# Other read places and directions for the feed-forward parts of a two-block transformer kernel

## The reference, cut to what matters

```python
# first block: 4 layers; mixers: retention, convolution, dilated attention, retention
x = x + _rmsnorm(m, norm_w[i, 1])
f = _swiglu(_rmsnorm(x, norm_w[i, 2]), ffn_w_in[i], ffn_w_out[i])   # hidden 2816
x = x + _rmsnorm(f, norm_w[i, 3])

def _swiglu(h, w_in, w_out):
    a = h @ w_in
    return (jax.nn.silu(a[..., :FFN_HIDDEN]) * a[..., FFN_HIDDEN:]) @ w_out

# second block: 2 layers on 16 + 256 = 272 tokens; mixers: mLSTM with LRU ("ab"), differential attention ("c")
h = h + mixer(_rmsnorm_2(h, norm_mix[layer]))
h = h + _sq_relu_mlp(_rmsnorm_2(h, norm_mlp[layer]), mlp_w1[layer], mlp_w2[layer])   # hidden 4096
```

## Time and profile before

| what | us |
|---|---|
| median of two timed runs | 2424.04 |
| lowest, highest | 2419.61, 2428.47 |
| span of the profiled execution | 2427.9 |
| instructions in it | 55624 |

### The profile page before, as it was taken

How to read it: one execution, slowest core, us unless ns; L and a number is a source line. 1 busy time by engine, 2 the same in 40 slices (tenths; PEclk the granted TensorE clock), 3 DMA queues, 4 the chain that set the end, 5 groups by cost and what they waited for, 6 DMA issues and landing times.

```text
span 2427.9 us, 55624 instructions
## 1 busy us (share of the span) xinstructions
PE 2388.4 (98%) x20004; PEld 2293.9 (94%) x20004; DVE 1705.2 (70%) x3359; ACT 1360.3 (56%) x2806; POOL 3.4 (0%) x9
## 2 busy tenths in 40 slices
PE   8999999999999999999999999999999999999998
PEld 8899999889999999999998999999899999999998
DVE  7667667877658777776576667657566775677764
ACT  5556555375555545565555555557755444566443
POOL 0000000000000000000000000000000000000000
PEclk9999999999999999999999999999999999999999
DMA  7535564336654444456555456644444555434564
GB/s 238 178 123 166 182 199 157 106 105 182 197 172 133 138 130 138 140 165 194 195 157 174 128 165 187 203 161 155 139 123 143 168 174 175 129 111 140 175 179 130
DMA packets 103400, 385.75 MB, mean 159 GB/s; under 512 B 11344, under 2 KB 13520, under 8 KB 103024
## 3 DMA queue, kind: packets, MB, share of 16 engines
q1 hardware_dynamic: 102784, 381.78, 50.5%
q0 software_dynamic: 496, 2.38, 0.3%
HBM read 383.07 MB, written 1.05 MB: 158 GB/s over the span
## 4 chain that ended last, share of the span: by engine, by line
PE 90%; DVE 6%; ACT 2%; issue 1%; DMA 0%; DVEq 0%; ACTq 0%; SPq 0%
PE acc L526 26%; PE acc L527 25%; PE acc L528 25%; DVE weights_lo L2155 2%; PE acc L732 1%; PE acc L733 1%; PE acc L734 1%; PE acc L754 1%; ACT weights_hi L1313 1%; PE acc L821 1%; PE acc L844 1%; PE acc L866 1%; DVE y L2293 1%; DVE h L2304 1%; PE acc L667 1%
## 5 line engine op out<-in xcount | busy, mean ns | idle before, releaser
L2155 DVE TENSOR_TENSOR weights_lo<-weights,weights_hi 128x512 fp32r<-128x512 f32 (+1 forms) x1392 | 907.0, 682 | 413.1 <-ACT weights_hi L1313 408.8
L526 PE MATMUL acc<-xn_parts,weights_hi 128*128 128x256 f32 (+1 forms) x3456 | 988.8, 286 | 14.3 <-DVE xn_parts L2300 6.8
L527 PE MATMUL acc<-xn_parts,weights_hi 128*128 128x256 f32 (+1 forms) x3456 | 974.7, 282 | 0.0
L528 PE MATMUL acc<-xn_parts,weights_lo 128*128 128x256 f32 (+1 forms) x3456 | 974.4, 282 | 0.0
L1313 ACT ACTIVATE weights_hi<-weights 128x512 fp32r<-128x512 f32 (+1 forms) x1392 | 815.6, 620 | 260.7 <-PE acc L528 230.8
L526 PEld LDWEIGHTS acc<-xn_parts,weights_hi 128*128 128x128 f32 x3456 | 653.7, 189 | 30.7 <-issue 21.8
L528 PEld LDWEIGHTS acc<-xn_parts,weights_lo 128*128 128x128 f32 x3456 | 652.3, 189 | 0.0
L527 PEld LDWEIGHTS acc<-xn_parts,weights_hi 128*128 128x128 f32 x3456 | 650.9, 188 | 0.9
L526 PE MATMUL acc<-arena_r,weights_hi 128*128 128x256 f32 (+1 forms) x1792 | 510.0, 285 | 3.6 <-DVE arena_r L2796 1.2
L528 PE MATMUL acc<-arena_r,weights_lo 128*128 128x256 f32 (+1 forms) x1792 | 506.3, 283 | 0.0
L527 PE MATMUL acc<-arena_r,weights_hi 128*128 128x256 f32 (+1 forms) x1792 | 506.2, 282 | 0.0
(11 more groups left out here) (325 smaller groups left out, 2324.5 us busy)
## 6 DMA issues: line engine op xcount, KB each, us to landing
weights<-in_ffn_in SPq DMA_DIRECT2D x176, 512.0 KB, 3.8
weights<-in_ffn_out SPq DMA_DIRECT2D x64, 704.0 KB, 4.1
weights<-in_att_in SPq DMA_DIRECT2D x72, 512.0 KB, 3.5
weights<-in_mlp_in SPq DMA_DIRECT2D x64, 512.0 KB, 3.5
weights<-in_mlp_out SPq DMA_DIRECT2D x64, 512.0 KB, 3.5
weights<-in_ret_qk SPq DMA_DIRECT2D x32, 512.0 KB, 3.7
weights<-in_ret_v SPq DMA_DIRECT2D x32, 512.0 KB, 3.6
weights<-in_ret_g SPq DMA_DIRECT2D x32, 512.0 KB, 3.6
```

The lines of the kernel that those rows point to most:

```text
L526: nc.tensor.matmul(acc, hi, src_hi, start=first, stop=False)
L527: nc.tensor.matmul(acc, hi, src_lo, start=False, stop=False)
L528: return nc.tensor.matmul(acc, lo, src_hi, start=False, stop=last)
L2155: nc.vector.tensor_tensor(w_lo[sub % phase.subs][:, 0:n, :], raw[slot][:, j * SUB:j * SUB + n, :], w_hi[sub % phase.subs][:, 0:n, :].bitca ...
```

## The change

The inputs of the feed-forward parts get places of their own, one for each layer, and six parts read them backwards.

```diff
-S2_STRIDE, MLP_AT, ARENA_PLACE = 320, 16, 832
+S2_STRIDE, ARENA_PLACE = 320, 832
+TURNED_INPUTS = ("ffn_in0", "ffn_out0", "ffn_in1", "mlp_in1", "mlp_out0", "mlp_out1")
+XN_AT = ((64, 64), (80, 80), (48, 80), (48, 96))
+XN2_AT = 48
+HIDDEN_AT = ((48, 48), (48, 48), (0, 16), (0, 32))
+MLP_AT = (0, 48)
...
-        xn_hi = {S1: chunks(xn_parts, 48, DC, S1), S2: chunks(xn_parts, 0, DC, S2_STRIDE)[:, :, 0:S2]}
...
+        def xn_place(number, half):
+            return (XN_AT[number // 2] if number % 2 else (48, 48))[half] + half * DC * S1
+
+        def xn_hi(number):
+            if number < 2 * DEPTH:
+                return chunks(xn_parts, xn_place(number, 0), DC, S1)
+            return chunks(xn_parts, 0, DC, S2_STRIDE)[:, :, XN2_AT:XN2_AT + S2]
...
-        hid_hi, hid_lo = chunks(arena_r, 0, FFN, S1), chunks(arena_r, FFN * S1, FFN, S1)
-        mlp_hi, mlp_lo = (chunks(arena_r, MLP_AT + n * MLP * S2_STRIDE, MLP, S2_STRIDE)[:, :, 0:S2] for n in range(2))
+        hid_hi = [chunks(arena_r, at[0], FFN, S1) for at in HIDDEN_AT]
+        hid_lo = [chunks(arena_r, at[1] + FFN * S1, FFN, S1) for at in HIDDEN_AT]
+        mlp_hi = [chunks(arena_r, at, MLP, S2_STRIDE)[:, :, 0:S2] for at in MLP_AT]
+        mlp_lo = [chunks(arena_r, at + MLP * S2_STRIDE, MLP, S2_STRIDE)[:, :, 0:S2] for at in MLP_AT]
...
-            def product(acc, hi, lo, src, first, last):
+            def product(acc, hi, lo, src, first, last, name=""):
                 src_hi, src_lo = src
+                if name in TURNED_INPUTS:
+                    acc, src_hi, src_lo = acc[:, ::-1], src_hi[:, ::-1], src_lo[:, ::-1]
                 nc.tensor.matmul(acc, hi, src_hi, start=first, stop=False)
```

More of the change, by code:

```diff
@@ L248, in chunks, with xn_lo @@
             return buf[:, at:at + n * t].rearrange("p (c t) -> p c t", t=t)
-        xn_hi = {S1: chunks(xn_parts, 48, DC, S1), S2: chunks(xn_parts, 0, DC, S2_STRIDE)[:, :, 0:S2]}
-        xn_lo = {S1: chunks(xn_parts, 48 + DC * S1, DC, S1),
-                 S2: chunks(xn_parts, DC * S2_STRIDE, DC, S2_STRIDE)[:, :, 0:S2]}
+        def xn_place(number, half):
[4 more added lines that the diff above has]
+            return chunks(xn_parts, 0, DC, S2_STRIDE)[:, :, XN2_AT:XN2_AT + S2]
+        def xn_lo(number):
+            if number < 2 * DEPTH:
+                return chunks(xn_parts, xn_place(number, 1), DC, S1)
+            return chunks(xn_parts, DC * S2_STRIDE, DC, S2_STRIDE)[:, :, XN2_AT:XN2_AT + S2]
         proj1 = chunks(arena, 0, 48, S1)
@@ L540, in multiply @@
                     last = product(acc, w_hi[sub % phase.subs][:, k % SUB, :], w_lo[sub % phase.subs][:, k % SUB, :], src(kk),
-                                   kk == 0, kk == phase.upo * phase.tiles - 1)
+                                   kk == 0, kk == phase.upo * phase.tiles - 1, phase.name)
                     if k % SUB == SUB - 1 or k == phase.tiles - 1:
@@ L597, in first_units @@
                         last = product(acc(u), w_hi[c % phase.subs][:, u, :], w_lo[c % phase.subs][:, u, :], src(c),
-                                       c == 0, c == DC - 1)
+                                       c == 0, c == DC - 1, phase.name)
                     last.then_inc(sub_multiplied, 1)
@@ L1269, in _ @@
                 gated_pairs(ph[f"ffn_in{layer}"], layer, src, ready)
-                src, ready = hidden(hid_hi, hid_lo, f"ffn_in{layer}")
+                src, ready = hidden(hid_hi[layer], hid_lo[layer], f"ffn_in{layer}")
                 dense_outputs(ph[f"ffn_out{layer}"], src, S1, ready)
@@ L1522, in chunk @@
                         act.wait_ge(x_ready, first - DC + c + 1)
-                    hi, value = xn_hi[S1][:, c, :], x[:, c, :]
+                    hi, value = xn_hi((k + 1) // 2)[:, c, :], x[:, c, :]
                     if residues:
@@ L2296, in rest @@
                     dve.wait_ge(xh_ready, DC * number + c + 1)
-                    lo, value, hi = xn_lo[S1][:, c, :], x[:, c, :], xn_hi[S1][:, c, :].bitcast(F32)
+                    lo, value, hi = xn_lo(number)[:, c, :], x[:, c, :], xn_hi(number)[:, c, :].bitcast(F32)
                     if residues:
@@ L2531, in unit @@
                     m = i * phase.body + u
-                    split_hidden(mlp_hi[:, m, :], mlp_lo[:, m, :], part[:, u % 2, :], i * phase.body, u, first)
+                    split_hidden(mlp_hi[int(phase.name[-1])][:, m, :], mlp_lo[int(phase.name[-1])][:, m, :], part[:, u % 2, :], i * phase.body, u, first)
                 stream(phase, unit)
```

20 lines of the change are left out of this document (10 added, 10 removed).

## The result

The kernel after takes 2444.39 us (2443.51 to 2445.27, two runs), the kernel before 2424.04 us; the ratio is 1.0080 with an interval of 1.0054 to 1.0107. It is slower by 20 us, inside the forecast range (2402 to 2458) and 16 us above the forecast of 2428.

A forecast was written before the change was run, and what follows sets the result against it. The prediction took TensorE's distance between matmul starts (121 ns over 20004 matmuls) to bound the kernel. Its terms 0 + 4 + 0 = +4 us on the median 2424.0 gave 2428 us, range 2402 to 2458 us.

The forecast's parts named there:

- (b): New places of the 272-column parts, 4800 matmuls: +0.8 ns each, +4 us, with ends of -24 and +7 us.
- (a): New places of the 256-column feed-forward parts, 6336 matmuls: a fresh draw of two levels, 0, with 14.6 us either side.
- they meet more often: Rival: in turned parts, moving and weight reads collide once more per matmul, +32 us, 2460 us; chance 0.15.
- the signs that the prediction named for being wrong: Turned or unequal-halves parts at their own level (turned 256 columns: below 112, above 119 ns), or 272-column parts at 64 falling towards 120.
- (c): Six parts read backwards, output too: 0 us, bounds from -9.7 and -11.8 us to near +496 us.
- No effect: Rival: places and direction don't matter, timing draws the levels of the parts; 2424 us, chance 0.15.
- The turned parts run free: Rival: turned ffn_in parts fall to 113.1 ns, turned MLP parts to 120.2; -21.5 us, about 2404 us; chance 0.18.
- Half pace: Rival: backward reading or writing in turned parts runs at half pace, (c)'s worst end, 2920 us; chance 0.07.

The follow-up runs named there:

- the experiment on the first block: Kernel after with the second block as before the change (forwards at 128), first block's places and directions kept: 2448.99 us, ratio 1.0112 to the kernel before.
- places alone: Kernel after with its new places but every part read forwards (no turned inputs): 2441.13 us, ratio 1.0082 to the kernel before.
- direction alone: Kernel after with its six parts still read backwards but all places put back as before the change: 2427.64 us, ratio 1.0030 to the kernel before.
- the backward map: Kernel after with all twelve feed-forward parts read backwards, at places 0, 64, 128 and 192 modulo 256 bytes; levels read, no time given.
- the padding: 64 bytes ahead of the weight buffers, against a kernel reading all parts forwards at 64; weights and xn shift, arena stays: 2432.34 us beside 2431.28 for the kernel before.
- the experiment on the rhythm: One plain f32 matmul heading each later ffn_in turn, added to the kernel with everything forwards at 64: 2417.71 us, ratio 0.9989 to the kernel before.

## Why the prediction was right or wrong

*The number* lies in the range and its sign is right, but that is in good part luck. Of the three terms of the sum, (b) had the wrong sign (+4 forecast, -5.6 measured in the two profiles), and (a), put at 0 with 14.6 us at most on either side, came to +19.4, outside its own bounds; the two misses partly cancel. That 2444 us fell inside 2402 to 2458 is owed to the room left for "they meet more often", whose mechanism did not occur. By the signs that the prediction named for being wrong, it was wrong: turned parts above 119 ns (120.0 in ffn_out0 and ffn_in1), a level of its own for halves at different places (118.7 in ffn_in3), and 272-column parts forwards at 64 down to 123.5 ns, part of the way towards 120.

*TensorE's distance between starts bounds the kernel, and nothing else moves*: right. Busy times, waits and clock of the other engines stayed, and every microsecond found is in that distance.

*Step (a), new places are a fresh draw with as many high as low, 0 us*: this step failed. I had seen that equal places show both levels and concluded that places don't matter. The runs show that both 113.3 and 117.8 ns were open at a distance of -64 bytes from the weights, and that the changed places held 117.8 to 120.0 ns in every long part. What it cost is all of the low parts and more: four parts from 113.3 to between 117.8 and 120.0 ns (+3.3 in ffn_out0, +2.6 in ffn_out1, +4.3 in ffn_in2, +5.2 us in ffn_in3, over their longest unbroken stretches), 0.6 and 2.1 us in ffn_in0 and ffn_in1, 19.4 us for the block in the two profiled executions. It is even more against the timed ones (27 to 29 us in the experiment on the first block). That fits a kernel before that is low in more parts in most of its runs than in the execution that I read: its medians of 2419 to 2420 us in the later measurements are close to the 2419.38 us of the execution with seven low parts. The levels of the timed runs themselves were not seen. That the profiled execution stood at the upper end of the timed pair was in the prediction; I did not ask what it was high by.

*Step (b), 272 columns +4 us*: wrong in sign. The price was taken from ab_out, whose chunks visit all four places (126.1 ns). That is within 0.6 ns of the mean of the four places (64 at 123.3, 128 at 125.3 or 126.7, 0 and 192 at 126.7); I used it for 64 alone. Measured: -5.6 us for the block, made of -1.8 ns a matmul in the parts that read forwards at 64, -0.3 to -0.4 ns in the two turned ones at 64, and 0 in mlp_out1.

*Step (c), direction 0 with bounds of -21.5 and +496 us*: right as a sum at the new places (places alone 1.0082, full change 1.0080), not as a rule. At the old places direction alone costs 1.0030, and seven out of seven long backward parts at 64 (three in that kernel, four in the backward map) stand on the high level.

*The rivals.* "No effect" fell: the padding moved levels as predicted by distance. "The turned parts run free" fell: none came below 117.8 ns. "They meet more often" had the first half of its criterion fulfilled, a turned 256-column part above 118 ns (118.3, 120.0, 120.0), and not the second, a turned 272-column part above 130 (125.0 to 125.3). Its idea that the moving read and the weight read hinder each other fits the dependence on their distance, but the unturned parts lost as much (places alone), so it is not about turning. "Half pace" fell altogether: the most that a long backward part took was 120.0 ns for 256 columns and 125.3 for 272.

*Two readings of rows.* 95/760 is 125.0 ns, not 124.9, which changes nothing. The 14 entries at L520 are not 14 matmuls: the kernel issues seven there (`keep_busy(7, 6)`), and in the experiment on the rhythm 36 plain f32 matmuls more gave 72 entries more (20076 against 20004). So 215 ns is the distance of two entries and some 430 ns that of two such matmuls, and the worst end of (c) should have been about three times 496 us. No row bears out either for a backward read.

*The two rules weighed beside the sum.* The rule of two independent read ports (the Trainium skill, "TensorE: Matmul & The Clock Gate", section "Step-by-step: what each phase is for") would, as I took it, have made every place equal. The padding run disagrees with that: moving the weights by 64 bytes took ffn_out0 to 118.7 ns with its input untouched, where it had 113.3 in every profile of the kernel before. Whether the two reads meet in the memory or elsewhere no run here shows. The Trainium skill's page "PSUM — Partial Sum Buffer", in its specifications, warns that non-contiguous patterns slow matmuls significantly; a backward output with a backward input shows no such slowing here, the MLP parts took 124.5 ns backwards at 128 where forwards they take 125.3 or 126.7. Input and output were turned together in every run, so what each does alone is not shown.

*What stays open*: what sets the level where two are open, at -64 bytes above all. The first block was low in 14 of 24 parts in the three profiles of the kernel before and in 24 of 24 in the three of the kernels with the second block forwards at 64 (one of them with the breaks), though what the first block reads and writes is the same in both; their timed difference of 8 us is no more than the second block alone accounts for. The kernel with the padding had two of its four ffn_in high at the same distance. The traces say that it isn't a toss of a coin for each part. ret_out0 and ret_out3, at that distance too, were high in all 13 profiles without the padding. In att_in of the kernel before, in each of seven turns of its loop and in all three profiles, 18 matmuls run at 113.3 ns, then 24 on the arena's weights at 120.0, then 24 at 117.8 that read the same places modulo 256 as the 18, without a break between; in the kernel with the padding the arena's 24 have 113.3 and the 24 behind them have it too. So what has gone before in the stream bears on the level. How, was not found.

## What to carry to other kernels

Where TensorE is never idle, look at the distance between starts in column times, part by part: a part at 288 instead of 272 for the same 256 columns is 6% of that part, and no busy share shows it. It can be had by placing the moving operand at the right distance from the weights modulo 256 bytes (here -64 was best for both widths); test each width, and profile more than once, since one place can hold two levels. A mean over places says nothing about one place, and one profiled execution says little about which level the timed runs have.

## What the runs showed of the hardware

- The distance between matmul starts in a steady stream of fp32r products takes a few values in column times: 272.0, 281.2, 282.7, 284.0, 284.8, 286, 288.0 for 256 columns; 296.0, 298.7, 300.0, 300.8, 304.0 for 272.
- It depends on the distance of the moving operand's place from that of the weights, modulo 256 bytes, and on the direction of the read; 16 bytes can cost 1.4 to 6 ns (64 against 48 and 80).
- Two of these values can belong to one set of addresses (113.3 and 117.8 ns at -64 and +64, 118.7 and 120.0 at -128), and each held for nearly a thousand matmuls of a long part. That accounts for most of the 17 us between the profiled spans of one program (2417.6 to 2435.0). A break need not change the level (36 of 36 turns came back to the low one), and weights at another place between can change it without a break (att_in).
- A backward read with a backward output stays near the pace of the stream: against forwards at the same place it stands between 2.2 ns below (192, 272 columns) and 2.2 ns above (192, 256 columns), or 4.5 above where forwards has its low level (64, 117.8 against 113.3).
- A plain f32 matmul leaves two entries in the trace (72 for 36), 216 ns apart for 256 columns at L520.
